# The first weight pair of each seven-product stage in the order in which its products read it, with two K pairs ahead of a barrier

## The chip, the cores and the metric

The kernel runs on one core of one Trainium2 chip. The time is the device time of one execution in microseconds. Five engines work side by side and wait for each other by semaphores: TensorE (PE) multiplies, VectorE (DVE), ScalarE (ACT) and GpSimd (POOL) do elementwise work, SyncE (SP) issues most DMAs. TensorE's clock is granted at one of two levels, 1.2 and 2.4 GHz (0.50 and 1.00 in the profile).

## The reference

One inference step of a two-layer encoder on 1024 prompt frames and 8 x 16 sample frames, 1152 tokens in all, width 1024. Each layer is a mixer and a SwiGLU FFN, each behind an RMSNorm and added to the residual x:

```python
def _rmsnorm(x, g):
    xf = x.astype(jnp.float32)
    y = xf * lax.rsqrt(jnp.mean(xf * xf, axis=-1, keepdims=True) + EPS)
    return (y * g.astype(jnp.float32)).astype(x.dtype)
...
def _swiglu(h, w_gu, w_down):
    gate, up = jnp.split(h @ w_gu, 2, axis=-1)
    return (jax.nn.silu(gate) * up) @ w_down
...
        x = x + y.astype(x.dtype)
        x = x + _swiglu(_rmsnorm(x, w['ffn_norm'][layer]), w['ffn_w_gu'][layer],
                        w['ffn_w_down'][layer]).astype(x.dtype)
```

Layer 0 mixes with gated DeltaNet and GLA and one output projection, layer 1 with chunked attention behind `h @ w['c_w_qkv']`.

## The kernel before

Activations are kept transposed: `xT` is 8 tiles of 128 rows by 1152 tokens. A float32 operand is split into a high part (a cast on ScalarE) and a low part (source minus high part, on VectorE for tokens and GpSimd for weights), and a product is three matmuls: high by high, low by high, high by low.

**Seven products.** The FFN's input projection (22 pairs of weight tiles, p = 0 to 21) and the QKV projection (12 pairs) are computed as 2 x 2 blocks in seven products instead of eight: pair p of the weights, halves of the contraction and of the 1152 tokens. Products 0 to 6 are a11 x11, S2 T2, S1 T1, S3 T3, a12 x21, a22 T4, S4 x22. S are sums of weight blocks, made by four additions on GpSimd (`make_sums`, lines 762 to 767) once a pair has come by DMA. T are sums of token blocks. A product runs over four K blocks i, of six matmuls of 288 columns each (`block_product`, line 864). `high_part` (line 774) and `low_part` (line 778) split block q of pair p; `wts.low` counts the low parts done, and each product waits for a count. A pair after the first takes 168 matmuls.

**The tokens.** For block i, VectorE makes T1 (line 567), T2 (580), T3 (583), T4 (586), and low parts of x11 (572), T2 and T1 (593). ScalarE scales x by the gain (551), after the save of x to DRAM has landed, and makes the high parts (555, 559, 563). The four later sources, products 3 to 6, are split by `high_late` (602, 604) and `low_t_late`, `low_x_late` (609, 614), four blocks each, while the first products run.

**The norm.** The sums of squares per token come by TensorE (`norm.sums`, line 466), a square root by ScalarE (`norm.root`, 483; at two of the joints behind a table load), the inverse by VectorE (`norm.invert`, 495), and three groups of matmuls spread the inverse over partitions (476), which ScalarE copies into `norm_row` (`keep_group`, 488). VectorE multiplies results by that row (lines 1516 to 1532 in the FFN, 2250 in QKV).

**Order.** Every engine runs its own instruction list, in the order in which the functions below write it; nothing is scheduled. Three joints are touched: `mixer_out` to the first FFN, with an all-engine barrier in it; the first FFN to `qkv_in_seven`; `project_add` to the second FFN. At the first, products 0 to 2 of pair 0 are computed ahead of the barrier but for the last K block of products 1 and 2, then `keep_warm(2)` (line 143). Behind the barrier, semaphores start with credits for what was done ahead. In an FFN pair, product 3 waits for `u2_done`, an addition on VectorE (1504) that stands in its list behind the previous pair's `finish`: a multiply (1536) that waits for ScalarE's silu (1353), and a low part (1538) that waits for its high part (1361). ScalarE casts the seven weight blocks of the next pair (`block(p, q)`) ahead of silu. In QKV the results of a V pair are turned by transposes between products (line 2079, up to six groups a pair), and ScalarE copies them out (2185), two copies ahead of the cast of the next pair's block 0 and two behind it. A pair's load is issued by SyncE when low part 5 of the pair before is done (line 753).

## Time and profile before

| | us |
|---|---|
| median of 3 runs | 3249.42 (3249.1 to 3250.72) |
| profiled execution | 3249.41 |
| its span, first to last instruction | 3247.8 |
| TensorE busy | 3092.3 (95%) |
| VectorE busy | 1584.2 (49%) |
| GpSimd busy | 1550.3 (48%) |
| ScalarE busy | 1038.1 (32%) |
| TensorE's mean granted clock | 0.977 |

A timeline row has start, duration, engine, line, operation, tiles, shapes, the count of merged instructions, and in brackets the idle time of the engine ahead of it with what ended it.

### The profile page before, as it was taken

The page shows a single profiled execution, that of the slowest core. Times are in us where ns is not written, and L with a number is a line of the kernel's source. Part 1 is how long each engine was busy: PE and PEld are TensorE (multiplying, and loading weights), DVE is VectorE, ACT ScalarE, POOL GpSimd, SP SyncE. Part 2 cuts the span into 40 slices and gives each one's busy share as a digit, 9 for nine tenths or more (in the row PEclk, how much of TensorE's full clock was granted, in tenths as well). Part 3 has the DMA queues.
Part 4 walks back from the last instruction along what each step waited for, and adds up shares of the span by engine and source line. Part 5 has one row for each costly group of instructions (what it writes and reads, how often), then busy time and mean ns, then how long its engine had stood idle before and what let it go on. Part 6 is the DMA issues. An engine that isn't in the chain of part 4 may idle for free. (4 is left out here: it accounts for less than half of the span.)

```text
span 3247.8 us, 67369 instructions
## 1 busy us (share of the span) xinstructions
PE 3092.3 (95%) x28530; PEld 2904.6 (89%) x28530; DVE 1584.2 (49%) x2179; ACT 1038.1 (32%) x1840; POOL 1550.3 (48%) x1182
## 2 busy tenths in 40 slices
PE   7999977888898999999999999999999999999998
PEld 6988866777798999999999999877699999999997
DVE  5650034655666545554334433466645545644323
ACT  4222132334334332231213432366524322231204
POOL 4452143444125776774363556211135776673454
PEclk8999988999899999999999999999999999999999
DMA  6222142432661322236433353566522323328241
GB/s 207 83 79 96 49 119 89 145 109 94 206 200 54 106 101 78 91 122 255 144 99 132 93 165 104 191 207 230 152 70 83 96 83 104 104 98 293 91 146 65
DMA packets 369352, 408.93 MB, mean 126 GB/s; under 512 B 28856, under 2 KB 303377, under 8 KB 368040
## 3 DMA queue, kind: packets, MB, share of 16 engines
q1 hardware_dynamic: 362216, 379.71, 35.3%
q0 software_dynamic: 6848, 25.04, 2.5%
q8 instruction: 222, 3.64, 0.5%
q14 instruction: 66, 0.54, 0.1%
HBM read 272.18 MB, written 134.60 MB: 125 GB/s over the span
## 5 line engine op out<-in xcount | busy, mean ns | idle before, releaser
L864 PE MATMUL PS<-token_block,w_block 128*128 128x288 f32 x9408 | 1269.1, 297 | 13.9 <-POOL w_block L778 6.5
L864 PEld LDWEIGHTS PS<-token_block,w_block 128*128 128x128 f32 x9408 | 1260.4, 189 | 16.8 <-POOL w_block L778 6.2
L778 POOL TENSOR_TENSOR w_block<-w_pair_raw,w_block 128x512 fp32r<-128x512 f32 x224 | 305.4, 1369 | 161.9 <-ACT w_block L774 127.9
L1267 PE MATMUL PS<-act_slot,w_down_split 128*128 128x384 f32 x1872 | 330.4, 337 | 5.1 <-DMA act_slot<-act_dram 4.0
L1267 PEld LDWEIGHTS PS<-act_slot,w_down_split 128*128 128x128 f32 x1872 | 328.1, 189 | 6.7 <-DMA act_slot<-act_dram 4.9
L778 POOL TENSOR_TENSOR w_block<-w_sum,w_block 128x512 fp32r<-128x512 f32 x168 | 229.6, 1380 | 94.0 <-ACT w_block L774 94.0
L774 ACT CAST w_block<-w_pair_raw 128x512 fp32r<-128x512 f32 x224 | 137.2, 621 | 309.0 <-PE PS L864 260.5
L774 ACT CAST w_block<-w_sum 128x512 fp32r<-128x512 f32 x168 | 99.3, 620 | 365.7 <-POOL w_sum L767 236.8
L1239 PE MATMUL PS<-token_block,w_block 128*128 128x288 f32 x1344 | 180.3, 296 | 2.7 <-issue 2.6
L1239 PEld LDWEIGHTS PS<-token_block,w_block 128*128 128x128 f32 x1344 | 179.4, 189 | 3.5 <-issue 3.0
L762 POOL TENSOR_TENSOR w_sum<-w_pair_raw 128x512 f32<-128x512 f32 x56 | 87.1, 1555 | 165.8 <-DMA w_pair_raw<-in_ffn_w_gu_dram 115.5
L405 PE MATMUL PS<-hT_high,w_split_tiles 128*128 128x384 f32 x576 | 125.0, 343 | 2.6 <-DVEq L2511 2.6
L1089 POOL CAST w_down_split<-w_down_raw 128x1024 fp32r<-128x1024 f32 (+2 forms) x32 | 28.1, 878 | 206.7 <-PE PS L1267 171.1
L1583 DVE TENSOR_TENSOR xT<-xT,PS 128x1152 f32<-128x1152 f32 x32 | 43.3, 1353 | 153.4 <-PE PS L1267 153.4
L1509 DVE TENSOR_TENSOR u<-p,PS 128x576 f32<-128x576 f32 x44 | 33.1, 751 | 159.6 <-PE PS L864 159.6
L4728 ACT ACTIVATE probs<-minus_scores,minus_max 128x640 f32<-128x640 f32 (+3 forms) x144 | 101.0, 705 | 23.1 <-DVE minus_max L4617 22.9
L3175 POOL TENSOR_TENSOR gla_k_exps<-gla_exps,gla_kT 128x896 f32<-128x896 f32 x18 | 37.0, 2079 | 145.3 <-ACT gla_exps L3595 145.3
L1574 DVE TENSOR_TENSOR xT<-xT,PS 128x576 f32<-128x576 f32 x72 | 52.6, 751 | 106.1 <-PE PS L1239 106.1
L405 PEld LDWEIGHTS PS<-hT_high,w_split_tiles 128*128 128x128 f32 x576 | 101.5, 191 | 2.9 <-POOLq L2381 2.9
L4765 POOL COPY bias_samples<-bias_near 128x384 f32<-128x384 f32 x16 | 8.1, 506 | 194.0 <-DMA bias_near<-near_dram 147.2
L764 POOL TENSOR_TENSOR w_sum<-w_sum,w_pair_raw 128x512 f32<-128x512 f32 x56 | 96.1, 1716 | 4.4
L1525 DVE TENSOR_TENSOR ffn_up<-ffn_up,norm_row 128x1152 f32<-128x1152 f32 x44 | 91.1, 2070 | 4.9 <-DVE ffn_up L1522 0.5
(467 smaller groups left out, 5557.8 us busy)
## 6 DMA issues: line engine op xcount, KB each, us to landing
w_pair_raw<-in_ffn_w_gu_dram SPq DMA_DIRECT2D x88, 512.0 KB, 5.1
act_slot<-act_dram SPq DMA_DIRECT2D x28, 1152.0 KB, 13.7
cache_kT<-kT_dram SPq DMA_DIRECT2D x8, 2048.0 KB, 11.0
cache_v<-in_cache_c_v_dram SPq DMA_DIRECT2D x64, 256.0 KB, 4.9
act_dram<-ffn_act_high SPq DMA_DIRECT2D x28, 576.0 KB, 2.8
act_dram<-ffn_act_low SPq DMA_DIRECT2D x28, 576.0 KB, 3.9
down_source<-down_dram SPq DMA_DIRECT2D x56, 288.0 KB, 5.0
xT<-xT_dram SPq DMA_DIRECT2D x24, 576.0 KB, 11.7
```

Of the source, the lines that this page charges most:

```text
L405: m = nc.tensor.matmul(PS[:, banks + j, 0:GN], wl if p == 2 else wh, sl if p == 1 else sh, start=(k == first and p == 0), stop=(k == last ...
L762: tt(self.sum_(p, 2), b0, b1, ALU.add).then_inc(self.summed, 1)
L764: tt(self.sum_(p, 1), self.sum_(p, 2), a0, ALU.subtract).then_inc(self.summed, 1)
L774: self.nc.scalar.copy(self.blocks[q][:, 0], self.source(p, q)).then_inc(self.high, 1)
L778: self.nc.gpsimd.tensor_tensor(self.blocks[q][:, 1], self.source(p, q), self.blocks[q][:, 0], ALU.subtract).then_inc(self.low, 1)
L864: m = nc.tensor.matmul(to[:, j], w, x[:, j * HN:(j + 1) * HN], start=(q < 3 and i == 0 and t == 0), stop=(q > 3 and i == 3 and t == 2), sk ...
L1239: m = nc.tensor.matmul(to[:, j], w, x[:, j * HN:(j + 1) * HN], start=(q < 3 and i == 0 and t == 0), stop=(q > 3 and i == 3 and t == 2), sk ...
L1267: m = nc.tensor.matmul(down_banks(u)[:, j], wd[u % 2][:, int(q == 2), k], x[:, int(q == 1), group(j)], start=(k == 0 and q == 0), stop=(k ...
L1525: tt(up[:], up[:], row[:], ALU.mult).then_inc(up_scaled, 1)
L1574: tt(two(x), two(x), down_tile(d, q), ALU.add).then_inc(x_down, 1)
L1583: tt(groups(xT[:, n]), groups(xT[:, n]), down_banks(u), ALU.add).then_inc(x_added, 1)
L4728: nc.scalar.activation(pr[:, g % 2, hp, 0:w], sc[:, hp, 0:w], ACT.Exp, scale=-1.0, bias=mn[:, g % 2, hp, 0:1], accum_out=sm[:, g % 2, hp, ...
```

## The change

- `make_rest` is split into `make_t2`, `make_t4` and `make_t3`, and `low_t` waits only for its own source. At every joint VectorE now goes T2, low T2, T4, low T1, T3 instead of T2, T3, T4, low T2, low T1.
- `norm.root` and `norm.invert` move ahead of the four high and low parts of product 5's source.
- ScalarE's cast of block 0 of pair 1 moves ahead of the `keep_group` copies, and GpSimd's low part of it ahead of the wait for x22's low parts and the sums of pair 1.
- In `mixer_out`, the sums of the first weight pair move ahead of square additions 2 and 3 on GpSimd; squares and weight casts are placed anew on ScalarE; VectorE takes adds 6 and 7 later.
- The last K block of products 1 and 2 (12 matmuls) moves ahead of the barrier.

```diff
     def low_t(self, dve, q, i):
         dve.wait_ge(self.high, 3 * i + (2 if q == 2 else 3))
-        dve.wait_ge(self.t_made, 4 * i + 4)
+        dve.wait_ge(self.t_made, 4 * i + (2 if q == 2 else 3))
...
         for q in wts.order[5:7]:
             wts.low_part(pool, 0, q)
+        wts.low_part(pool, 1, 0)
         tok.wait_late(pool, 6)
         for p in range(1, NP):
             wts.make_sums(pool, p)
-            for q in range(7):
+            for q in range(int(p == 1), 7):
                 wts.low_part(pool, p, q)
...
+        norm.root(act)
         for i in range(4):
             tok.high_late(act, 5, i)
-        norm.root(act)
         act.wait_ge(wts.low, 7)
         for i in range(4):
             tok.high_late(act, 6, i)
+        block(1, 0)
         for j in range(G):
             norm.keep_group(act, j)
-        for q in range(6):
+        for q in range(1, 6):
             block(1, q)
...
         middle(0)
+        norm.invert(dve)
         for i in range(4):
             tok.low_t_late(dve, 5, i)
-        norm.invert(dve)
...
     def pe_credits(pe):
-        pe.sem_inc(mm, 1)
+        pe.sem_inc(mm, 3)
...
-        for n in (1, 2, 3):
+        add_square(1)
+        pool.wait_ge(mm, LAST * KT + 2)
+        wts.make_sums(pool, 0)
+        for n in (2, 3):
             add_square(n)
         wts.low_part(pool, 0, 0)
-        pool.wait_ge(mm, LAST * KT + 2)
-        wts.make_sums(pool, 0)
...
         block_product(nc, pe, tok, wts, half_banks(PS, 0), 0, 0, range(3, 4))
+        block_product(nc, pe, tok, wts, half_banks(PS, 2), 0, 2, range(3, 4))
+        block_product(nc, pe, tok, wts, half_banks(PS, 1), 0, 1, range(3, 4))
         e.keep_warm(2)
...
-        for i in range(3):
+        for i in range(4):
             square(LAST, 2 * i)
-            square(LAST, 2 * i + 1)
-            if i == 2:
-                act.wait_ge(mm, LAST * KT + 7)
+            if i == 3:
                 for q in wts.order[1:3]:
                     wts.high_part(act, 0, q)
             act.wait_ge(x_squared, LAST * KT + 2 * i + 1)
             tok.scale(act, i)
             tok.high_x11(act, i)
-            tok.high_t1(act, i)
-            tok.high_t2(act, i)
             if i == 1:
                 act.wait_ge(mm, LAST * KT + 3)
                 wts.high_part(act, 0, 0)
-        square(LAST, 6)
-        act.wait_ge(x_squared, LAST * KT + 7)
-        tok.scale(act, 3)
-        tok.high_x11(act, 3)
-        tok.high_t1(act, 3)
+            if i < 3:
+                square(LAST, 2 * i + 1)
+            tok.high_t1(act, i)
+            tok.high_t2(act, i)
+        square(LAST, 7)
         for q in wts.order[3:5]:
             wts.high_part(act, 0, q)
-        tok.high_t2(act, 3)
-        square(LAST, 7)
...
         for i in range(4):
             if 0 < i < 3:
                 add(LAST, 2 * i)
-            if i < 3:
-                add(LAST, 2 * i + 1)
+            add(LAST, 2 * i + 1)
+            tok.make_t1(dve, i)
+            dve.wait_ge(added, LAST * KT + 2 * i + 2)
+            tok.make_t2(dve, i)
+            tok.low_x11(dve, i)
+            tok.low_t(dve, 2, i)
+            tok.make_t4(dve, i)
+            tok.low_t(dve, 1, i)
             if i == 2:
                 add(LAST, 6)
-            tok.make_t1(dve, i)
-            tok.low_x11(dve, i)
-            if i == 2:
-                add(LAST, 7)
-            dve.wait_ge(added, LAST * KT + 2 * i + 2)
-            tok.make_rest(dve, i)
-            tok.low_t(dve, 2, i)
-            tok.low_t(dve, 1, i)
+            tok.make_t3(dve, i)
```

ScalarE at the first joint ahead of the barrier, before: squares (line 4318), casts of weight blocks 1 and 2 from `w_sum`, then scale (551) and high parts of token block i = 2, then square 6.

```order
L4318 ACTIVATE x_sq_2795<-xT 128x384 x2
L774 CAST w_block_2764<-w_sum 128x512
L774 CAST w_block_2765<-w_sum_2771 128x512
L551 ACTIVATE xT<-xT,gains 128x1152
L555 CAST token_block_2728<-xT 128x576
L559 CAST token_block_2736<-token_sum_2760 128x576
L563 CAST token_block_2732<-token_sum_2756 128x576
L4318 ACTIVATE x_sq_2795<-xT 128x384
```

The same stretch of ScalarE's list after the change, from square 4 to scale 3.

```order
L4334 ACTIVATE x_sq_2795<-xT 128x384
L551 ACTIVATE xT<-xT,gains 128x1152
L555 CAST token_block_2728<-xT 128x576
L4334 ACTIVATE x_sq_2795<-xT 128x384
L559 CAST token_block_2736<-token_sum_2760 128x576
L563 CAST token_block_2732<-token_sum_2756 128x576
L4334 ACTIVATE x_sq_2795<-xT 128x384
L778 CAST w_block_2764<-w_sum 128x512
L778 CAST w_block_2765<-w_sum_2771 128x512
L551 ACTIVATE xT<-xT,gains 128x1152
```

The two casts stood ahead of scale 2 and now stand behind square 6, just ahead of scale 3.

GpSimd at the first joint behind the barrier, before: low parts of blocks 5 and 6 of pair 0, the four sums of pair 1, low parts of pair 1 (`w_block` without a number is block 0).

```order
L778 TENSOR_TENSOR w_block_2768<-w_pair_raw,w_block_2768 128x512
L778 TENSOR_TENSOR w_block_2769<-w_sum_2772,w_block_2769 128x512
L762 TENSOR_TENSOR w_sum_2774<-w_pair_raw 128x512
L764 TENSOR_TENSOR w_sum_2773<-w_sum_2774,w_pair_raw 128x512
L765 TENSOR_TENSOR w_pair_raw<-w_pair_raw 128x4x128
L767 TENSOR_TENSOR w_sum_2775<-w_pair_raw,w_sum_2773 128x512
L778 TENSOR_TENSOR w_block<-w_pair_raw,w_block 128x512
L778 TENSOR_TENSOR w_block_2764<-w_sum_2773,w_block_2764 128x512
```

The same place in GpSimd's list after the change.

```order
L782 TENSOR_TENSOR w_block_2768<-w_pair_raw,w_block_2768 128x512
L782 TENSOR_TENSOR w_block_2769<-w_sum_2772,w_block_2769 128x512
L782 TENSOR_TENSOR w_block<-w_pair_raw,w_block 128x512
L766 TENSOR_TENSOR w_sum_2774<-w_pair_raw 128x512
L768 TENSOR_TENSOR w_sum_2773<-w_sum_2774,w_pair_raw 128x512
L769 TENSOR_TENSOR w_pair_raw<-w_pair_raw 128x4x128
L771 TENSOR_TENSOR w_sum_2775<-w_pair_raw,w_sum_2773 128x512
L782 TENSOR_TENSOR w_block_2764<-w_sum_2773,w_block_2764 128x512
```

The low part of block 0 of pair 1 moved from behind the four sums to ahead of them; the other two joints read alike.

## Rows read from the trace of the kernel before

**Rows 1.** The page's engine table: busy us (share of the span) xinstructions.

```profile
PE 3092.3 (95%) x28530; PEld 2904.6 (89%) x28530; DVE 1584.2 (49%) x2179; ACT 1038.1 (32%) x1840; POOL 1550.3 (48%) x1182
```

**Rows 2.** TensorE's waits, whole span: us in total, times, longest.

```profile
PE PS L864 <- POOL w_block L778: 6.5, 4, 1.8
...
PE PS L476 <- DVE norm_by_token L495: 3.7, 3, 1.2
```

**Rows 3.** Timeline of TensorE, first joint.

```profile
1004.68 3.92 PE L864 MATMUL PS<-token_block,w_block 128*128 128x288 f32 x18 [2.90 <-DVE token_block L572]
...
1012.92 1.88 PE L143 MATMUL PS<-consts_f 128*128 128x512 f32 x4
1018.94 3.00 PE L864 MATMUL PS<-token_block,w_block 128*128 128x288 f32 x12 [4.14 <-DVEq L1723]
...
1024.12 6.64 PE L864 MATMUL PS<-token_block,w_block 128*128 128x288 f32 x48
...
1042.47 17.76 PE L864 MATMUL PS<-token_block,w_block 128*128 128x288 f32 x120 [1.85 <-POOL w_block L778]
```

**Rows 4.** Timeline of ScalarE, first joint.

```profile
977.51 1.26 ACT L551 ACTIVATE xT<-xT,gains 128x1152 f32<-128x1152 f32 x1 [1.19 <-DMA xT_dram<-xT]
...
986.76 1.26 ACT L551 ACTIVATE xT<-xT,gains 128x1152 f32<-128x1152 f32 x1 [0.93 <-DMA xT_dram<-xT]
...
998.98 1.14 ACT L774 CAST w_block<-w_sum 128x512 fp32r<-128x512 f32 x2 [2.25 <-POOL w_sum L767]
```

**Rows 5.** Timeline of VectorE, first joint ahead of the barrier.

```profile
982.92 1.43 DVE L593 TENSOR_TENSOR token_block<-token_sum,token_block 128x576 fp32r<-128x576 f32 x2 [0.46 <-DVE xT L586]
984.26 1.01 DVE L4366 TENSOR_TENSOR xT<-xT,PS 128x384 f32<-128x384 f32 x2
...
991.81 3.43 DVE L593 TENSOR_TENSOR token_block<-token_sum,token_block 128x576 fp32r<-128x576 f32 x2
...
1015.16 2.03 DVE L593 TENSOR_TENSOR token_block<-token_sum,token_block 128x576 fp32r<-128x576 f32 x2
```

**Rows 6.** Timeline of GpSimd, first joint behind the barrier.

```profile
1034.88 1.30 POOL L762 TENSOR_TENSOR w_sum<-w_pair_raw 128x512 f32<-128x512 f32 x1 [6.08 <-DVE token_block L614]
```

**Rows 7.** The chain that ended last, third joint: start, us, what.

```profile
2467.80 2.87 DVE token_block L614 x4
...
2475.89 2.35 POOL w_block L778
...
2488.17 11.83 PE PS L864 x87
```

**Rows 8.** Timeline of VectorE, third joint.

```profile
2484.97 2.39 DVE L1538 TENSOR_TENSOR ffn_act_low<-ffn_gate,ffn_act_high 128x1152 fp32r<-128x1152 f32 x1 [1.23 <-ACT ffn_act_high L1361]
2487.29 0.74 DVE L1504 TENSOR_TENSOR u<-p,PS 128x576 f32<-128x576 f32 x1
```

**Rows 9.** Timelines of TensorE, ScalarE and GpSimd, second joint.

```profile
1816.71 4.96 PE L864 MATMUL PS<-token_block,w_block 128*128 128x288 f32 x24 [1.84 <-POOL w_block L778]
...
1830.08 0.79 PE L2079 MATMUL PS<-consts_f,xT 128*128 128x128 f32 x5 [0.61 <-ACT xT L2185]
...
1829.15 0.62 ACT L774 CAST w_block<-w_pair_raw 128x512 fp32r<-128x512 f32 x1 [5.83 <-DMA w_pair_raw<-in_c_w_qkv_dram]
...
1819.62 3.75 POOL L778 TENSOR_TENSOR w_block<-w_pair_raw,w_block 128x512 fp32r<-128x512 f32 x3
```

**Rows 10.** Timeline of VectorE, first joint behind the barrier.

```profile
1022.51 0.75 DVE L1504 TENSOR_TENSOR u<-p,PS 128x576 f32<-128x576 f32 x1
...
1051.42 0.74 DVE L1504 TENSOR_TENSOR u<-p,PS 128x576 f32<-128x576 f32 x1
```

**Rows 11.** Stretch table: stretch, its us, busy by engine, granted clock, DMA.

```profile
1044.50:1046.50 2.00, 2.00 (x10) 2.00 (x10) 0.62 (x1) 1.34 (x2) 2.00 (x2) 0.50 0.00 0
```

**Rows 12.** DMA issues, 2460 to 2500 us: count, KB each, median us to landing.

```profile
w_pair_raw<-in_ffn_w_gu_dram SPq DMA_DIRECT2D x4, 512.0 KB, 5.0
```

**Rows 13.** Timeline of SyncE's DMA issues, third joint.

```profile
2464.08 23.09 SPq L753 DMA_DIRECT2D w_pair_raw<-in_ffn_w_gu_dram  x4
```

More of the change, by code:

```diff
@@ L1150, in first_pair @@
                 product(0, 2, (0, 1, 2))
-            product(0, 1, (3,))
-            product(0, 2, (3,))
-            if not seam.begun:
+                product(0, 1, (3,))
+                product(0, 2, (3,))
                 seam.wait_squares(pe)
@@ L1667, in vector @@
                 dve.wait_ge(x_added, KT + 2 * i + 2)
-                x2.make_rest(dve, i)
+                x2.make_t2(dve, i)
                 x2.low_t(dve, 2, i)
+                x2.make_t4(dve, i)
                 x2.low_t(dve, 1, i)
+                x2.make_t3(dve, i)
             add_square(KT - 1)
@@ L2056, in gpsimd @@
             wts.make_sums(pool, p)
-            for q in range(7):
+            for q in range(int(p == 1), 7):
                 wts.low_part(pool, p, q)
@@ L2194, in scalar @@
             wts.high_part(act, 0, q)
+        norm.root(act)
         for i in range(4):
             tok.high_late(act, 5, i)
-        norm.root(act)
         act.wait_ge(wts.low, 7)
@@ L2200, in scalar @@
             tok.high_late(act, 6, i)
+        block(1, 0)
         for j in range(G):
             norm.keep_group(act, j)
-        for q in range(6):
+        for q in range(1, 6):
             block(1, q)
@@ L2278, in vector @@
         middle(0)
+        norm.invert(dve)
         for i in range(4):
             tok.low_t_late(dve, 5, i)
-        norm.invert(dve)
         for i in range(4):
```

33 lines of the change are left out of this document (20 added, 13 removed).

## The prediction

> **What bounds the kernel now.** I read the engine table of the page first: TensorE is busy 95% of the span [rows 1], so a change is worth what it does to TensorE's gaps and clock and no more. Then the list of waits. The change touches three joints, where one stage hands over to a stage of seven products: the first at 977 to 1054 us (mixer output to the first FFN, with the barrier in it), the second at 1809 to 1830 (FFN to QKV), the third at 2467 to 2488 (attention output to the second FFN). At each the list shows the same two gaps: about 1.2 us before the spread of the inverse roots (3.7 in three) and 1.8 us before the first product of pair 1, which waits for a low part from GpSimd (6.5 in four, one of them elsewhere); once there is a barrier gap of 4.1 [rows 2, 3]. Those are what the edits go at. Last I read the timelines of all engines through the joints, asking at each which wait ends last, because a gap that closes early only helps if nothing behind it is tied to another engine.
>
> **First joint, ahead of the barrier.** Now: the last mixer product ends at 1000.1, TensorE waits 2.9 us for the low part of x11 block 2, computes 48 block matmuls, warms for 1.9 and is done at 1014.8 [rows 3]. VectorE is the last to arrive (1015.16 + 2.03 = 1017.2 [rows 5]); TensorE restarts at 1018.94 [rows 3], so the barrier costs 1.75 after the last arrival.
>
> I lay the new order out with durations of rows: 0.72 to 0.8 us for a VectorE operation on a 576-wide half (two in 1.43), 1.7 if GpSimd works beside it (two in 3.43), 0.5 for an add [rows 5]; 1.26 for a scale, 0.68 for a high part, 0.57 for a weight cast [rows 4]; 1.3 for a GpSimd operation [rows 6], 1.6 beside VectorE.
> - GpSimd's four sums, which ran at 992.8, now follow square 1. ScalarE takes that square behind scale 0 and its high part (977.5 + 1.3 + 0.7 [rows 4]), so the sums run at about 981 to 988. They meet VectorE in block 0, which was then uncontended: five operations go from 0.75 to about 1.6. Adds 2 and 3, at 984.3 now [rows 5], come at 988.2.
> - Scale 1 waits for the save of x that this add releases, some 2 us (984.7 to 986.76 [rows 4, 5]): 990.7. Block 1's seven VectorE operations, three beside GpSimd's low part and squares, end at 998.9; adds 4 and 5 at 999.8; scale 2 again waits for its save, 1001.4. T2 stands ahead of the low part of x11, so block 2 of a11 x11 is ready at 1005.7 (1004.68 now).
> - The decisive move: the casts of weight blocks 1 and 2 ran at 998.98 [rows 4], ahead of scale 2. They now stand behind square 6, which waits for add 6, which VectorE takes only after the low part of T1 in block 2: add 6 at 1008.4, square 1008.9, two casts 1010.0, two low parts 1012.4. The products S2 T2 and S1 T1 both wait for that. TensorE has nine block steps left, 54 matmuls of 0.135 us (48 in 6.64 [rows 3]) and about 1.4 more at the half clock after the wait (12 matmuls took 3.00 instead of 1.6 after the barrier gap [rows 3]): 1021.1, and 1.9 of warming: 1023.0. The last arrival moves from 1017.2 to 1023.0: **+5.8 us**. The two moved K pairs (12 matmuls) are in this.
> Bounds: with no slowing between VectorE and GpSimd the same layout ends at 1016.4, a gain of 0.8; with operations of both slowed as in the worst pair of rows it ends 1 us later, +6.8. I stay at 5.8, since the 3.43 us for two [rows 5] is from this very stretch.
>
> The Trainium skill (SBUF — State Buffer, Who interferes with whom) says that a VectorE instruction with two SBUF inputs and a GpSimd instruction that reads SBUF exclude each other for a whole instruction. The 3.43 us agree roughly; full alternation by that rule would put the end another 1 to 2 us later.
>
> **Behind the barrier, first joint.** The sums of squares follow at once, but product 3 waits for u2, which was ready 4.3 us behind the restart (1022.51 + 0.75 - 1018.94 [rows 3, 10]; casts, low parts, the add) and will be again, so of the 3.0 us of moved matmuls only about 0.8 are gained there. The root and the inverse are then early, the 1.2 us gap goes; low part (1,0) is early, and the 1.85 us gap [rows 3] goes. But product 3 of pair 1 waits for its u, and that hangs on another chain: last low part of x22 to four GpSimd sums (1034.88 on [rows 6]) to six casts, table load, silu, multiply, high part, low part and u at 1051.42 + 0.74 = 1052.2 [rows 10]. TensorE reached that product at 1042.47 + 17.76 - 6.7 = 1053.5 [rows 3], so the slack is only 1.35 us. The chain does not get shorter. GpSimd takes low part (1,0) as soon as the weights have landed and are cast, about 1033.5 if the load takes 5 us as at the third joint [rows 12], and ends about when the sums could start; and VectorE's multiplications by the norm row, which fell on GpSimd's low parts (2.35 instead of 1.29, [rows 7]), now fall on the sums: +1.1 and +0.5. Less 0 to 0.9 for a low part that may run uncontended, u is ready 0.6 to 1.5 later; the joint ends 0 to +0.1 against now, and TensorE then has a gap of 2 to 3 us before the product. A gap of 1.85 brought the granted clock to 0.50, the 1.2 GHz level, for about 3 us [rows 3, 11]; now this price is paid at the first product of pair 1, later at the fourth, perhaps on top of one at the second. I take **+1.0** (0 to 1.8).
>
> **Third joint.** The same chain without slack: low parts of x22 end at 2470.67, sums at 2475.89 [rows 7]; low part 2.39, u at 2487.29 + 0.74 = 2488.03 [rows 8]; TensorE's product starts at 2488.17 [rows 7]. Weights of pair 1 land 5 us (the median) after their issue at 2464.1 and about 0.5 later [rows 12, 13], near 2469.7. Then cast and low part (1,0) occupy GpSimd till about 2471.8: the sums start 1.1 later, and meet the two multiplications, +1.6 at most; the low part of the activations runs freer, -0.9. u comes 1.8 later. A new gap of some 3 us before the product costs between nothing and 1.4 in clock. **+2.2** (+1 to +4).
>
> **Second joint.** There is no silu here, but TensorE's fifth transpose group waits for a row copy behind the cast of pair 2's first block, which waits for its load (1829.15, released by the DMA); TensorE waits 0.61 [rows 9]. The load is issued once GpSimd has done low part (1,5), at 1819.62 + 3.75 = 1823.4 [rows 9]. GpSimd's operations to there are the same ten, but the sums start some 0.8 late behind low part (1,0) (an estimate from the third joint, whose loads take the same 5 us), wait 0.6 for a cast behind them, and the low part taken ahead, 1.3, goes off the end: load about +0.3 with the stretching by VectorE the same. TensorE's earlier arrival turns into about 4.5 us of waiting, and the half clock behind it (24 matmuls in 4.96 for 3.3, [rows 9], paid at pair 1 now and included in today's arrival) is paid again behind the wait: **+1.8** (0 to +2.3).
>
> Orders of T2, T4, T3 in the second and third joint cost nothing: TensorE runs 72 block matmuls there without a gap; the cover is gone only if the low part of T1 moved by more than some 3 us, and it moves forward.
>
> **Sum.** 5.8 + 1.0 + 2.2 + 1.8 = +10.8 us. The profiled execution took 3249.41 (span 3247.8), the median is 3249.42, so they can be used alike: 3260.2.
>
> **Rivals.**
> - *Light contention at the first joint* (0.20): sums and VectorE overlap little, as the 1.3 us rows on GpSimd would allow; the barrier moves by 0 to 2.5 instead of 5.8; 3250 to 3256, centre 3254.
> - *Gaps close and nothing replaces them* (0.07), on the other side. The mechanism is the low part (1,0) in pair 1: if the weights land so early that it ends before the low parts of x22, and if the chain to u has 2 us more room than I read, TensorE keeps 1.2 + 1.8 us a joint and about 1.5 of clock at two. That gives -12, and with the barrier coming 5.8 later, -6; with a neutral barrier 3238. It decides for faster where u in pair 1 is done before TensorE's third product ends.
> - *Worse* (0.08): half clock after each of TensorE's new waits ahead of the barrier and behind it, 3265 to 3270.
> - *No change* (0.03): the last arrival at the barrier stays VectorE's.
> The forecast itself has 0.62, with a range of its own of 3255 to 3264.
>
> **Numbers.** Range 3253 to 3265: the forecast, most of the light rival; left out are the worse one's end and the faster side. What a measurement here tells from no change is 0.2%, 6.5 us. Slower by more, from 3255.9: 0.59 of the forecast, 0.05 of the light rival, 0.08 of the worse one, 0.72. The same: 0.03, 0.14 and no change's 0.03, 0.20. Faster: 0.01 of the light rival and 0.07, 0.08.
>
> **What would show it.** The first matmul of S2 T2 at about 1012 instead of 1006; the restart behind the barrier near 1024.7; gaps before the spread and before pair 1 gone; new waits of TensorE, on VectorE's u at the fourth product of pair 1 (first and third joint), on ScalarE's row copy at the second. I am wrong if the casts of blocks 1 and 2 are done by 1004, or if TensorE enters the fourth product without a wait.

## The result, and the profile after

The changed kernel took 3267.99 us, the median of 8 runs (3257.4 to 3269.62), against 3249.26 for the kernel before beside it (8 runs, 3238.78 to 3255.41): a ratio of 1.0061, 95% interval 1.0046 to 1.0075. It is slower, as forecast, and by more than the range allowed (3253 to 3265). The profiled execution took 3267.39 us, its span 3265.8, and TensorE was busy for 3094.8 us of it (3092.3 before [rows 1]); the loss is waiting, and clock.

Where TensorE waits at the joints (all of the span: us in total, times, longest):

```profile
PE PS L868 <- POOL w_block L782: 12.5, 5, 5.3
...
PE PS L868 <- DVE u L1509: 5.8, 2, 2.9
...
PE PS L2091 <- ACT xT L2197: 4.4, 1, 4.4
```

The wait for the inverse [rows 2] is gone from the list, the waits for `w_block` have doubled, and two new ones have come: for u, and for ScalarE's row copy (`xT` at line 2197). Timeline of TensorE through the first joint:

```profile
1006.22 1.06 PE L868 MATMUL PS<-token_block,w_block 128*128 128x288 f32 x6 [4.10 <-DVE token_block L572]
1012.57 9.72 PE L868 MATMUL PS<-token_block,w_block 128*128 128x288 f32 x54 [5.30 <-POOL w_block L782]
1022.13 1.88 PE L143 MATMUL PS<-consts_f 128*128 128x512 f32 x4
1025.73 2.14 PE L466 MATMUL PS<-consts_f,norm_row 128*128 128x1 f32 x18 [1.72 <-PEq L114]
1030.15 8.68 PE L868 MATMUL PS<-token_block,w_block 128*128 128x288 f32 x48 [2.28 <-issue]
...
1043.77 6.62 PE L868 MATMUL PS<-token_block,w_block 128*128 128x288 f32 x48
1052.95 6.64 PE L868 MATMUL PS<-token_block,w_block 128*128 128x288 f32 x48 [2.56 <-POOL w_block L782]
1062.50 3.69 PE L868 MATMUL PS<-token_block,w_block 128*128 128x288 f32 x16 [2.91 <-DVE u L1509]
```

S2 T2 starts behind a wait of 5.3 us; the restart behind the barrier is the row at 1025.73; product 3 waits 2.28 us for u2, and the 48 matmuls of products 3 and 4, one row, then take 8.68 us where they took 6.64 [rows 3]. The row at 1043.77 is product 6 of pair 0 and the first product of pair 1, which begins at 1047.0 without a gap; pair 1 waits for 2.56 us before its second product and 2.91 before its fourth (24 matmuls a product). VectorE and ScalarE ahead of the barrier, one timeline:

```profile
979.18 1.57 DVE L572 TENSOR_TENSOR token_block<-xT,token_block 128x576 fp32r<-128x576 f32 x1
980.68 1.85 DVE L597 TENSOR_TENSOR token_block<-token_sum,token_block 128x576 fp32r<-128x576 f32 x1
982.45 1.84 DVE L584 SCALAR_TENSOR_TENSOR xT<-xT,gains,token_sum 128x576 f32<-128x576 f32 x1
984.39 1.66 DVE L597 TENSOR_TENSOR token_block<-token_sum,token_block 128x576 fp32r<-128x576 f32 x1
985.98 1.85 DVE L590 SCALAR_TENSOR_TENSOR xT<-xT,gains 128x576 f32<-128x576 f32 x1
987.75 1.00 DVE L4376 TENSOR_TENSOR xT<-xT,PS 128x384 f32<-128x384 f32 x2
...
1008.34 0.55 DVE L4376 TENSOR_TENSOR xT<-xT,PS 128x384 f32<-128x384 f32 x1
...
1009.35 1.12 ACT L778 CAST w_block<-w_sum 128x512 fp32r<-128x512 f32 x2
...
1010.83 1.25 ACT L551 ACTIVATE xT<-xT,gains 128x1152 f32<-128x1152 f32 x1 [0.36 <-DMA xT_dram<-xT]
...
1018.36 1.85 DVE L590 SCALAR_TENSOR_TENSOR xT<-xT,gains 128x576 f32<-128x576 f32 x1
```

Five operations of block 0 take 1.57 to 1.85 us each beside GpSimd's first square addition and four sums (978.8 to 987.2), adds 2 and 3 come at 987.75, add 6 at 1008.34, and behind its square the two casts of blocks 1 and 2. VectorE's last operation ends at 1020.2, nearly four us ahead of TensorE's warming (1022.13 + 1.88). The second and third joint, timelines of TensorE:

```profile
1842.43 1.30 PE L2091 MATMUL PS<-consts_f,xT 128*128 128x128 f32 x5 [4.44 <-ACT xT L2197]
...
2496.94 6.66 PE L868 MATMUL PS<-token_block,w_block 128*128 128x288 f32 x48 [2.40 <-POOL w_block L782]
...
2506.48 1.78 PE L868 MATMUL PS<-token_block,w_block 128*128 128x288 f32 x6 [2.89 <-DVE u L1509]
```

**How executions are compared here.** Absolute times shift from execution to execution by more than the change is worth: the first joint starts between 965 and 976 us, though no edit stands ahead of it. The kernel before alone was timed at 3230 to 3262 us in the runs beside the experiments. So I measure inside each joint. In the first, zero is VectorE's first `xT<-xT,PS` addition of the last token group (970.98 in the first execution of the kernel before, 969.68 after); "the restart" is TensorE's first matmul behind the barrier; "behind" is from there to u3 of pair 4 (u3 is the second addition into `u`, line 1509 before, and product 5 waits for it). The second joint is from the first matmul of pair 0 to the eight transposes behind pair 2's run of 120 matmuls, the third from the first matmul of pair 0 to u3 of pair 4. Each is the difference of two rows.

| kernel | restart | last to arrive | behind | ratio, 95% |
|---|---|---|---|---|
| before, two executions | 47.96, 47.75 | VectorE 46.2, 46.0 | 105.3, 108.4 | |
| changed | 56.05 | TensorE 54.3 | 108.8 | 1.0061 (1.0046-1.0075) |
| 1 mixer part alone | 55.90 | TensorE 54.2 | 106.8 | 1.0017 (0.9995-1.0040) |
| 2 all but the mixer part | 47.54 | VectorE 45.8 | 112.0 | 1.0007 (0.9991-1.0023) |
| 3 casts 1, 2 back | 54.19 | TensorE 52.5 | 106.6 | 1.0021 (1.0005-1.0036) |
| 4 no early low part | 56.20 | TensorE 54.5 | 107.1 | 1.0020 (1.0009-1.0030) |
| 5 casts 1, 2 and sums back | 52.62 | TensorE 50.9 | 110.0 | 1.0031 (1.0016-1.0046) |
| 6 before + 12 matmuls ahead | 53.60 | TensorE 51.9 | 106.5 | 1.0019 (1.0007-1.0031) |
| 7 before + early root | 47.74 | VectorE 46.0 | 105.7 | 1.0004 (0.9984-1.0024) |
| 8 changed + warming | 55.63 | TensorE 53.9 | 106.3 | 1.0031 (1.0019-1.0042) |
| 9 12 matmuls back | 53.84 | TensorE 52.1 | 106.7 | 1.0040 (1.0018-1.0062) |
| 10 casts 1, 2, sums, 12 back | 52.45 | GpSimd 50.7 | 110.3 | 1.0036 (1.0013-1.0058) |
| 11 add 6 back | 52.60 | TensorE 50.9 | 109.7 | 1.0027 (1.0007-1.0046) |
| 12 add 6 and 12 back | 51.98 | GpSimd 50.2 | 106.8 | 1.0028 (1.0014-1.0043) |
| 13 as 10, add 6 back too | 50.73 | GpSimd 48.9 | 110.7 | 1.0007 (0.9987-1.0026) |
| 14 as 13, casts 3, 4 back too | 50.71 | VectorE 49.0 | 104.4 | 1.0014 (0.9987-1.0040) |
| 15 before, T3 behind barrier | 47.05 | VectorE 45.3 | 107.6 | 0.9993 (0.9976-1.0010) |
| 16 before, more warming | 47.69 | VectorE 45.9 | 105.7 | 0.9991 (0.9976-1.0006) |
| 17 both | 47.25 | VectorE, TensorE 45.5 | 106.4 | 0.9990 (0.9975-1.0006) |

Arrivals are counted like the restart, from the first add; each ratio is to the kernel before timed beside that kernel. In every row the restart is 1.72 to 1.78 us behind the last of the four arrivals. That makes the column of arrivals the thing to read: it names the engine that set the barrier. Kernels 5, 1 and 2 show that the ratios alone would not do: restarts of 52.6, 55.9 and 47.5 stand beside 1.0031, 1.0017 and 1.0007, with intervals that overlap.

### The profile page after: what moved, and what is told of

It reads as the page before. It is cut to its first block and busy times, and to the rows that moved or that the text cites. A ratio compares the mean times of both kernels' runs of the same rounds, so it can differ in the third digit from the quotient of the medians.

```text
span 3265.8 us, 67368 instructions
## 1 busy us (share of the span) xinstructions
PE 3094.8 (95%) x28530; PEld 2908.7 (89%) x28530; DVE 1590.4 (49%) x2179; ACT 1036.9 (32%) x1840; POOL 1544.1 (47%) x1182
## 5 line engine op out<-in xcount | busy, mean ns | idle before, releaser
L782 POOL TENSOR_TENSOR w_block<-w_pair_raw,w_block 128x512 fp32r<-128x512 f32 x224 | 295.0, 1322 | 188.2 <-ACT w_block L778 152.0
L1579 DVE TENSOR_TENSOR xT<-xT,PS 128x576 f32<-128x576 f32 x72 | 52.6, 751 | 106.1 <-PE PS L1243 106.1
```

The lines of the kernel that those rows point to most:

```text
L782: self.nc.gpsimd.tensor_tensor(self.blocks[q][:, 1], self.source(p, q), self.blocks[q][:, 0], ALU.subtract).then_inc(self.low, 1)
L1579: tt(two(x), two(x), down_tile(d, q), ALU.add).then_inc(x_down, 1)
```

## The experiments

**Before again.** The kernel before, unchanged.

> The kernel before, unchanged, for a second execution in the trace. Theory E (how long the granted clock stays at 0.50 behind a gap differs from execution to execution of one and the same list): the half clock behind the barrier, 3.4 us in the first execution, has another length here, up to the 10 us seen with the old part ahead of the barrier in the changed kernel. Rival F (the lists decide it): 3 to 4 us again, and the stretch from the restart to the fifth u3 is 105.3 us again.

Its TensorE timeline behind the barrier:

```profile
1015.82 2.83 PE L864 MATMUL PS<-token_block,w_block 128*128 128x288 f32 x12 [3.99 <-DVEq L1723]
1018.45 3.83 PE L466 MATMUL PS<-consts_f,norm_row 128*128 128x1 f32 x18
1022.15 8.60 PE L864 MATMUL PS<-token_block,w_block 128*128 128x288 f32 x48
```

Stretch table of the same execution (us, TensorE busy, granted clock, DMA):

```profile
1016.00:1018.00 2.00, 2.00 (x11) 0.59 0.04 8
1022.00:1024.00 2.00, 2.00 (x10) 0.50 0.00 0
1025.00:1027.00 2.00, 2.00 (x11) 0.60 0.54 152
```

The same list that ran products 3 and 4 in 6.64 us [rows 3] runs them here in 8.60: the clock stays at 0.50, the 1.2 GHz level, for 10.2 us instead of 3.4, and "behind" is 3.1 us longer. Theory E holds. A single trace therefore can't say that products 3 and 4 at half clock belong to the change. The two executions were taken at different times, but kernels 13 and 14 below, timed side by side and with one list behind the barrier, differ in the same way: 8.79 and 6.63 us for these 48 matmuls.

**1 and 2, the mixer part alone, and all but it.** Kernel 1 is the kernel before with the change's part ahead of the barrier; kernel 2 is the changed kernel with the old part.

```diff
 # kernel 2, against the changed kernel
-        block_product(nc, pe, tok, wts, half_banks(PS, 2), 0, 2, range(3, 4))
-        block_product(nc, pe, tok, wts, half_banks(PS, 1), 0, 1, range(3, 4))
         e.keep_warm(2)
...
```

> The kernel before with the first joint's part ahead of the barrier taken from the change (order of sums, squares, casts, adds, the 12 moved matmuls), all else as before. Theory A (late casts set the barrier, and TensorE's wait for u2 plus the half clock behind it delays the chain to u of pair 1): restart behind the barrier 26.0 us behind the first add of the last group (56.0 in the changed kernel, 48.0 before, counted from 970), a wait of about 2.3 us ahead of product 3 of pair 0 and 48 matmuls in 8.7 us behind it; whole kernel +9 to +11 us. Rival B (what was lost behind the barrier comes from the early low part and root): the 12 matmuls moved ahead give back about 0.8, product 3 runs at full clock, 6.6 us; whole kernel +7 us.

> The changed kernel with the old part ahead of the barrier (12 matmuls behind the barrier again). Theory A: the restart stands as in the kernel before, product 3 of pair 0 is entered without the wait for u2 and at full clock (48 matmuls in 6.6 us); behind the barrier the first joint costs +0.5 to +1.5, the second +2, the third +2.5; whole kernel +5 to +6 us. Rival B: the first joint costs +3.5 behind the barrier here too, whole kernel +8 us.

Kernel 1 restarts at 55.90, and kernel 2 at 47.54: all 8 us ahead of the barrier are the mixer part's. In kernel 1 the 48 matmuls of products 3 and 4 run in 8.59 us behind the 2.28 wait, as A says; but kernel 2, with no wait for u2, ran them in 8.42 at a half clock of 10.2 us, which A excluded, so the wait is not needed for it:

```profile
1030.04 8.42 PE L868 MATMUL PS<-token_block,w_block 128*128 128x288 f32 x48
```

That was why the kernel before was traced again. Whether the wait makes it likelier is open: with the 12 matmuls ahead of the barrier and no warming added, all seven executions took 7.9 to 8.8 us for these 48; with the 12 behind it, seven of twelve took 8.1 to 9.4 and five 6.5 to 6.6. The whole kernels can't tell A from B: the intervals of 1.0017 and 1.0007 reach from -2 to +13 and from -3 to +7 us.

**3 and 5, casts back, then sums back too.** ScalarE's casts of blocks 1 and 2 ahead of scale 2; then GpSimd's sums behind square additions 2 and 3.

```diff
-            if i == 3:
+            if i == 2:
+                act.wait_ge(mm, LAST * KT + 7)
                 for q in wts.order[1:3]:
                     wts.high_part(act, 0, q)
```

> The changed kernel with only the casts of weight blocks 1 and 2 put back ahead of ScalarE's scale 2. Theory A (these casts are what holds S2 T2): S2 T2 is entered without the 5.3 us wait, at 1006 to 1008, VectorE becomes the last to arrive (about 1020), and the restart moves from 1025.7 to 1021 to 1022; whole kernel 4 to 5 us shorter than the changed one, +4 to +7 against before. Rival C (VectorE and GpSimd slow each other, and the joint is late for that alone): the casts give at most 1 us.

> The changed kernel with the casts of weight blocks 1 and 2 ahead of scale 2 and GpSimd's four sums of pair 0 behind square additions 2 and 3 and the low part, both as before; VectorE's new order and the moved 12 matmuls stay. Theory C (the early sums slow VectorE's first blocks, and that remains once the casts are back): adds 2 and 3 return from 18 to 13.5 us behind the first add of the last group, the restart from 54.2 to 47 to 49 us behind it (47.96 before); whole kernel 5 to 7 us shorter than with the casts alone. Rival G (VectorE's own new order of T2, low parts and adds is what is slow): the restart stays above 52.

TensorE in kernel 3:

```profile
1009.46 9.38 PE L868 MATMUL PS<-token_block,w_block 128*128 128x288 f32 x48 [1.06 <-POOL w_block L782]
1020.13 1.06 PE L868 MATMUL PS<-token_block,w_block 128*128 128x288 f32 x6 [1.30 <-DVE token_block L597]
```

Theories A and C both missed. The wait ahead of S2 T2 shrinks from 5.3 to 1.06 us in kernel 3, but the restart moves by 1.9 and not by about 4: TensorE then waits again, at its last six matmuls, for the low part of T1 of the last block. With the sums back, adds 2 and 3 return to 13.6 and the restart moves by another 1.6 only, to 52.62, not to 47 to 49; that is rival G's "above 52", though the 12 matmuls are in it too. The late casts are one of several holds of nearly the same length.

**6 and 9, the 12 matmuls alone, and all but them.**

> The kernel before with only the 12 block matmuls of products 1 and 2 moved ahead of the barrier. The restart stays at 48 us behind the first add of the last group, since TensorE has 2.4 us to spare there. Theory A: the 3.0 us saved behind the barrier turn into a wait for u2 of about 2.3 us and half clock behind it; product 3 starts at most 0.8 us earlier and ends 0 to 1.5 us later than before; whole kernel 0 to +2 us. Rival H (the move is a gain that the other edits hide): no half clock, whole kernel -1 to -3 us.

> The changed kernel with only the 12 matmuls back behind the barrier. Theory N (two mechanisms overlap: the late casts hold TensorE to 1020 by themselves, the moved matmuls need VectorE's last low parts and would hold it nearly as long): the restart comes 53.5 to 55 us behind the first add of the last group (56.05 with both, 53.6 with the 12 matmuls alone, 47.96 without either), so each alone costs some 6 us and both together 8. Rival P (the 12 matmuls are nearly all of it): 48 to 50.

TensorE in kernel 6, where nothing else is changed:

```profile
1015.05 3.25 PE L864 MATMUL PS<-token_block,w_block 128*128 128x288 f32 x12 [3.44 <-DVE token_block L593]
1018.10 3.39 PE L143 MATMUL PS<-consts_f 128*128 128x512 f32 x4
1023.22 2.75 PE L466 MATMUL PS<-consts_f,norm_row 128*128 128x1 f32 x18 [1.73 <-PEq L114]
```

I had written that TensorE has 2.4 us to spare there, and expected the restart to stay at 48. It has them, and can't use them: the last K block of S2 T2 and S1 T1 needs VectorE's last low parts, its last operation ahead of the barrier (1013.64 + 2.03 = 1015.67). So these 12 matmuls and the warming behind them come after VectorE, at half clock (3.25 and 3.39 us instead of 1.6 and 1.88), and TensorE is the last to arrive, at 51.9 instead of 43.8. Alone the move costs 5.7 us at the restart. Behind it product 3 starts at 4.42 us and not at 5.18 or 6.32, as told for u2; to u3 of pair 4 it is 106.5, between the 105.3 and 108.4 of before, so a gain there can't be read. Kernel 9 shows that the other edits without it cost 5.9 to 6.1: theory N, two holds that overlap, and together make 8.

**10, 13 and 14, down to VectorE's order.** From the changed kernel with casts 1 and 2, sums and the 12 matmuls as before (10), to add 6 ahead of T1 of block 2 again (13), to the casts of blocks 3 and 4 between the high parts of T1 and T2 of the last block (14). The diff is add 6's move, in 13 and 14.

```diff
             add(LAST, 2 * i + 1)
+            if i == 2:
+                add(LAST, 6)
             tok.make_t1(dve, i)
...
             tok.low_t(dve, 1, i)
-            if i == 2:
-                add(LAST, 6)
             tok.make_t3(dve, i)
```

> The changed kernel with sums, casts and the 12 matmuls all as before in the first joint; only VectorE's order and the rest of ScalarE's stay new there. Theory Q (the new order of VectorE is harmless ahead of the barrier): restart at 47 to 49 us behind the first add of the last group. Rival R (it delays VectorE's last operation by itself, since T3 of the last block and adds 6 and 7 stand later): 50 or above.

> The kernel with sums, casts of blocks 1 and 2 and the 12 matmuls as before, and add 6 as before too; VectorE's order of T2, T4, T3 and low parts, the squares and the casts of blocks 3 and 4 stay new. Theory W (several chains of like length end at the barrier, each edit lengthens one, and the longest counts): T1 of the last block starts at about 40.0 behind the first add of the last group (42.6 with add 6 late, 38.2 before), GpSimd ends last at about 48.1, restart at 49.5 to 50.3. Rival X (the early sums are not in it): 51.5 or above.

> The same with the casts of weight blocks 3 and 4 back between the high parts of T1 and T2 of the last block. Theory W: GpSimd's last addition ends 1 to 1.4 us earlier, VectorE is the last to arrive again, restart at 48.3 to 49.3 (47.75 to 47.96 before). Rival Y (GpSimd's arrival is not what sets it): as e16.

There "e16" is kernel 13.

Kernel 10, timeline of ScalarE, VectorE and GpSimd:

```profile
1007.45 0.55 DVE L4375 TENSOR_TENSOR xT<-xT,PS 128x384 f32<-128x384 f32 x1
...
1009.96 1.25 ACT L551 ACTIVATE xT<-xT,gains 128x1152 f32<-128x1152 f32 x1 [1.40 <-DMA xT_dram<-xT]
...
1011.24 0.76 DVE L567 TENSOR_TENSOR token_sum<-xT 128x576 f32<-128x576 f32 x1 [2.04 <-ACT xT L551]
...
1017.81 1.50 POOL L4275 TENSOR_TENSOR norm_row<-norm_row,x_sq 128x384 f32<-128x384 f32 x1
```

Rival R of kernel 10 holds: the restart is at 52.45, though nothing but VectorE's order, the squares and the casts of blocks 3 and 4 are new. Here the route of add 6 is seen whole: add 6 at 1007.45, the save of that tile, scale 3 released by the DMA at 1009.96, T1 of the last block at 1011.24 behind 2.04 us of waiting. And GpSimd is the last to arrive (1017.81 + 1.50), because the casts of blocks 3 and 4 stand behind square 7 and its two low parts behind them. With add 6 back (13) the last block starts 1.7 us earlier (40.9 behind the first add) and the restart is 1.7 earlier, at 50.73, 0.4 above what theory W allowed and below rival X. With casts 3 and 4 back too (14) GpSimd is done 1.3 us earlier, and nothing is gained: its low parts now meet VectorE's last block, and VectorE is the last, at 49.0. I had expected 48.3 to 49.3; it is 50.71. What stays, 2.8 us, goes with VectorE's new order, and with ScalarE's new order of squares and high parts, which no kernel here puts back alone. Kernel 14, timeline of VectorE, T1 of block 2 and T1 of block 3:

```profile
1004.66 0.76 DVE L567 TENSOR_TENSOR token_sum<-xT 128x576 f32<-128x576 f32 x1 [3.43 <-ACT xT L551]
...
1013.90 0.74 DVE L567 TENSOR_TENSOR token_sum<-xT 128x576 f32<-128x576 f32 x1
```

That is 9.24 us for block 2 where it took 8.05 (30.33 to 38.38 behind the first add); block 2 also starts 1.35 us later, and the last block takes 0.2 longer: together the 2.8. How much of it is which engine's order isn't shown.

**11 and 12, add 6 back alone, and with the 12 matmuls back.**

> The changed kernel with only VectorE's add 6 back ahead of T1 of block 2. Theory S (add 6 releases the save of x tile 6, the save releases scale 3, and scale 3 starts all of the last token block; square 6 and the two casts stand in the same line): scale 3 starts at 35 to 37 us behind the first add of the last group instead of 41.2, S2 T2 is entered with at most 1 us of waiting, and what is left is the price of the 12 moved matmuls, which wait for VectorE's last low parts: restart at 51 to 53.6 instead of 56.05. Rival T (the loss is spread over contention and order): 55 or above.

> The same with the 12 matmuls back behind the barrier too. Theory S: nothing that matters is left of the loss ahead of the barrier although sums, casts, squares and the order of T2, T4, T3 and low parts are all as changed: restart at 47.5 to 49.5 (47.75 and 47.96 before). Rival T: 52 or above.

Kernel 11, timeline of ScalarE (scale 3) and TensorE:

```profile
1003.85 1.25 ACT L551 ACTIVATE xT<-xT,gains 128x1152 f32<-128x1152 f32 x1
...
1006.85 9.09 PE L868 MATMUL PS<-token_block,w_block 128*128 128x288 f32 x54 [2.04 <-POOL w_block L782]
...
1015.77 1.88 PE L143 MATMUL PS<-consts_f 128*128 128x512 f32 x4
```

Scale 3 starts 4.1 us earlier (37.1), S2 T2 is entered 2.8 earlier, still behind a wait of 2.04 where theory S had at most 1, and the restart comes at 52.60, within theory S's 51 to 53.6: of all single edits that were put back, this one takes back most, 3.5 of 8.1 us. But T1 of the last block starts at 42.5 as in the changed kernel (42.4): VectorE comes to it no sooner, since the early sums have made it late from block 0 on (adds 2 and 3 at 18.0, 13.3 before). So the gain went through the casts, which stand behind square 6, and not through scale 3: the number was hit by another route than theory S's. Kernel 12 misses its 47.5 to 49.5: GpSimd is the last again, with VectorE close behind. Timeline of VectorE, GpSimd and TensorE in kernel 12:

```profile
1014.40 1.82 DVE L590 SCALAR_TENSOR_TENSOR xT<-xT,gains 128x576 f32<-128x576 f32 x1
...
1015.56 1.50 POOL L4275 TENSOR_TENSOR norm_row<-norm_row,x_sq 128x384 f32<-128x384 f32 x1
...
1018.84 1.86 PE L868 MATMUL PS<-token_block,w_block 128*128 128x288 f32 x12 [2.79 <-DVEq L1731]
```

Against kernel 13 (50.73), kernel 12 has the early sums and the late casts of blocks 1 and 2: 1.25 us.

**4 and 7, the early low part of pair 1 taken out, and the root and the inverse alone.**

```diff
 # kernel 4, against the changed kernel
-        wts.low_part(pool, 1, 0)
...
-            for q in range(int(p == 1), 7):
+            for q in range(7):
...
-        block(1, 0)
```

> The changed kernel without the early cast and low part of block 0 of pair 1, at all three joints. Theory A (that low part delays the four sums and with them u of pair 1): the wait of 1.8 us ahead of pair 1 is back, the sums start 1.1 us earlier at the third joint, the wait for u shrinks from 2.9 to 0 to 1; third joint +0.5 to +1 instead of +2.7, second 0 to +1 instead of +2.1; whole kernel 2 to 4 us shorter than the changed one. Rival D (the multiplications that now meet the sums are what lengthens the chain): u comes no earlier, the gap of 1.8 comes on top, and the kernel takes 0 to 3 us longer than the changed one.

> The kernel before with only the root and the inverse moved ahead of the four high and low parts of product 5's source, at all three joints. Theory L (pair 1 is pinned by GpSimd's four sums, whatever TensorE gains ahead of them): the 1.23 us gap before the spread is gone, the gap before pair 1 grows from 1.8 to 3.0 or more, pair 1 starts 29.8 to 30.3 us behind the start of pair 0 at the third joint as before (29.6 to 29.8), and u of pair 1 comes 0.5 to 1.3 us later than the 38.6 to 38.8 of before, since the inverse stands ahead of the low parts that release the sums; whole kernel 0 to +3 us. Rival M (a closed gap is time won): pair 1 starts at 28.5 at the third joint, whole kernel -3 us.

TensorE at the third joint in kernel 4, the first product of pair 1:

```profile
2494.92 5.37 PE L868 MATMUL PS<-token_block,w_block 128*128 128x288 f32 x27 [3.76 <-POOL w_block L782]
```

The same place in kernel 7:

```profile
2477.03 5.25 PE L864 MATMUL PS<-token_block,w_block 128*128 128x288 f32 x27 [3.75 <-POOL w_block L778]
```

With the root and the inverse early the gap before the spread is gone in both, and the gap before pair 1 has grown from 1.76 to 3.75: pair 1 starts 30.3 us behind pair 0, against 29.6 to 29.8. Nothing is won, theory L, and the whole kernel 7 stays where it was (1.0004). Theory A of kernel 4 had this gap at 1.8 again; the wait for u behind it is gone, as it said. Counted from the first matmul of pair 0, u of pair 1 starts at 38.6 to 38.8 in the seven executions with the old lists there, at 40.0 in kernels 4 and 7, and at 40.9 to 41.8 with everything: 1.3 us are the early inverse and root, 1.3 the early low part. Kernel 4 has the new order of T2, T4 and T3 and kernel 7 the old one, so that order costs nothing there. At the second joint the early low part is all of the loss: kernel 4 takes 59.91 us there, as before (59.99), the changed one 62.11.

**8, 16, 15 and 17, the clock, and a try at something better.** Kernel 8 puts warming matmuls in the wait for u2; 16 doubles the warming of the kernel before; 15 moves T3 of the last block behind the barrier; 17 does both.

```diff
 # kernel 15, against the kernel before
+        if seam.begun:
+            tok.make_t3(dve, 3)
         for i in range(4):
             tok.low_t_late(dve, 3, i)
...
 # kernel 16, against the kernel before
-        e.keep_warm(2)
+        e.keep_warm(4)
```

> The changed kernel with four records (1.88 us) of warming matmuls behind the sums of squares, in the place of most of the 2.28 us wait for u2 ahead of product 3. Theory A (that wait is what lowers the clock for product 3): the 48 matmuls go in 6.6 to 7.2 us instead of 8.68, and the joint ends 1.5 to 2 us earlier. Rival J (the clock has fallen already for the barrier's gap and the 18 narrow matmuls behind it): product 3 takes 8 us or more again.

> The kernel before with eight records of warming ahead of the barrier instead of four (3.8 us instead of 1.9), so that TensorE is done at 45.8 behind the first add of the last group, still before VectorE (46.2), and the gap shrinks from 4.1 to 2.2. Theory U (the gap brings the clock down): no half clock behind the barrier, the 12 matmuls in 1.7 instead of 3.0, product 3 in 6.6, the stretch from the restart to the fifth u3 103 to 104 us instead of 105.3 to 108.4. Rival V (the 18 narrow matmuls behind the barrier bring it down too): half clock of 3.4 us or more again.

> The kernel before with one operation moved: VectorE's T3 of the last block, 1.89 us beside GpSimd and not read before product 3, goes from ahead of the barrier to the first place behind it. If VectorE is the last to arrive and its list decides, the restart comes 0.8 to 1.9 us earlier than 47.96 behind the first add of the last group, u2 comes at most 0.4 us later relative to the restart, which product 3 does not wait for, and the whole kernel is 1 to 2 us shorter, which the traces can show and the times hardly. Rival: what is saved ahead is a longer wait for the sums of pair 1, or TensorE's warming is the last to arrive: 0.

> The kernel before with T3 of the last block moved behind the barrier and eight records of warming: restart at 46.5 to 47.3, gap 1.75 to 2.2 us. Theory U: as for the run with the warming alone, so 2 to 5 us faster than before over the joint. Rival V: only the 0.9 us of T3.

In kernel 8 products 3 and 4 take 7.30 us: between the two answers, with a half clock that was over sooner (3.4 us), which one execution can't tell from chance. The added warming itself ran at half clock, 3.66 us, and put product 3 off by 0.3. TensorE behind the barrier in kernel 16:

```profile
1019.90 3.25 PE L864 MATMUL PS<-token_block,w_block 128*128 128x288 f32 x12 [2.45 <-DVEq L1723]
```

And in kernel 17:

```profile
1012.55 1.85 PE L882 MATMUL PS<-token_block,w_block 128*128 128x288 f32 x12 [1.77 <-DVEq L1743]
1014.23 2.06 PE L466 MATMUL PS<-consts_f,norm_row 128*128 128x1 f32 x18
1017.11 9.35 PE L882 MATMUL PS<-token_block,w_block 128*128 128x288 f32 x48 [0.81 <-issue]
```

Theory U falls: the gap went from 4.1 to 2.45 and 1.77 us, and the clock fell all the same, at once in 16, and in 17 in the further gap of 0.81 us ahead of product 3. T3 behind the barrier does what it should, the restart is 0.7 to 0.9 us earlier in kernel 15, and u2 0.1 later. The three kernels lie at 0.9990 to 0.9993 with intervals that take in 1: not slower, and not shown to be faster.

## Why the prediction was right and wrong

Averaged over the executions that share the lists in question, the terms are: at the restart 47.75 (before, before again, 2, 7: 47.5 to 48.0) to 55.95 (changed, 1, 4, 8: 55.6 to 56.2), **+8.2** for a forecast of +5.8; behind it 106.56 (before, before again, 7, 15, 16) to 108.39 (changed, 2, 3, 5 and 8 to 14), **+1.8** for +1.0, where single executions reach from 104.4 to 112.0; second joint 60.06 (before, before again, 1, 6, 15 to 17) to 62.01 (the same eleven), **+2.0** for +1.8; third joint, the same kernels, 112.24 to 113.60, **+1.4** for +2.2. The sum is 13.3 us where 10.8 was forecast. Only the restart and the second joint repeat closely enough to be read to a few tenths; for "behind" and the third joint the two means differ by 1.8 and 1.4 with a 95% interval (an estimate from the scatter of the executions) of about 2.0 and 1.4 either way. (Kernels 7 and 15, in the mean for "behind", have one edit there each.)

- **The restart is the term that failed**: +5.8 was forecast, 8.2 measured. In the changed kernel itself the path was the one told, late casts, S2 T2, 54 matmuls, warming; its steps were mis-sized. The five operations of block 0 took 1.57 to 1.85 us and not 1.6, so adds 2 and 3 came at 18.1 behind the first add (forecast 17.2), add 6 at 38.7 (37.4), and the first matmul of S2 T2 at 42.9 (41.4). The 54 matmuls took 9.72 us, not 8.7: 1.4 us had been set aside for the clock, and it stood at 0.50 for the first 5 us of them.
- **What it was put down to** failed too: "the decisive move: the casts" named one hold out of several. Put back alone they return 1.9 us; the 12 matmuls alone cost 5.7. I had counted their own 1.6 us ("in this") and put the wait for VectorE's last low parts at nothing. In the changed kernel that wait is covered, since those low parts are done before TensorE comes to them; it counts as soon as the casts are back. I followed the latest chain to its end, and not the next one below it.
- **The slowing of VectorE beside GpSimd** was right in kind. The operations of block 0 that took 0.7 to 0.8 us take up to 1.85. The Trainium skill (SBUF — State Buffer, Who interferes with whom) has a VectorE instruction with two SBUF inputs and a GpSimd instruction that reads SBUF contend for a shared port pair, which is an exclusive lock. By that rule, the trace agrees in kind: VectorE's 1.85 is its own 0.81 and 1.04 of a GpSimd operation of 1.30 [rows 6], not the whole of it. I had kept full alternation, "another 1 to 2 us", out of the sum; S2 T2 started 1.5 late.
- **Behind the barrier** the steps stood as told: u2 was ready 4.3 us behind the restart (3.57 + 0.75 in nearly all executions), 0.8 us were gained up to product 3, the gaps before the spread and before pair 1 went, and TensorE waited 2.91 us at the fourth product of pair 1. Not in the sum was that products 3 and 4 would run at half clock. The run of before again shows that they do so without the change as well; of the 3.4 us seen between the first two traces the means leave 1.8. (The recorded 0.6 to 1.5 for u should read 0.7 to 1.6 by its own terms: 1.1 + 0.5, less 0 to 0.9.)
- **Joints two and three** went by the named mechanism: 4.44 us for the row copy ("about 4.5"), 2.89 for u ("some 3"). u came 2.6 us later and not 1.8: 1.3 by the low part for a forecast of 1.1, and 1.3 by root and inverse where 0.7 was left for the multiplications; but the first execution of the kernel before had no half clock behind its gap before pair 1, which the other executions mostly have, so the joint as a whole lost less, 1.4.
- **The rivals.** *Light contention* is out by the five slowed operations, *no change* by TensorE's arrival behind VectorE's, *gaps close and nothing replaces them* because u in pair 1 is not done before TensorE wants it in any kernel with the early low part (waits of 1.4 to 2.9 us). *Worse*, with 0.08, is the one whose 3265 to 3270 holds the measured time, and its mechanism is seen in part: in the changed kernel's profiled execution the clock falls to 0.50 in the wait ahead of S2 T2, at u2, at u in pair 1, at the row copy and at u in the third joint, 30.6 us at half clock in the three joints against 13.6 and 20.5 in the two executions of the kernel before. What these cost is inside the terms above; it doesn't add to them.

**Left open.** The joints sum to 13.3 us, and by them alone the kernel would take some 3263 us, inside the stated range; the timed ratio says 15 to 24. So the restart's 2.4 us are nearly all by which the joints exceed the forecast sum, and they don't explain why the timed median lies at 3268. In the two profiled executions the span grew by 18.0 us: 8.1 at the restart, 3.4 behind it, 2.1 and 3.7 at the second and third joint, and 0.7 net in all other stretches; the terms behind the restart and of the third joint lie above their means. Kernel 8, the changed kernel with one warming call more (four records), was timed at 1.0031 (6 to 14 us), which fits the joints better, and kernels 1 and 2, whose edits together are the change, at 1.0017 and 1.0007. The eight timed runs of the changed kernel list a mean granted clock of 0.974 to 0.976, kernel 8's ten 0.972 to 0.978 with a mean 0.002 higher, so the clock may be part of it; that isn't shown. Where the changed kernel's other 5 us were I can't place.

## What to carry to other kernels

Ahead of a barrier, list the arrival of every engine and not only of the last: here TensorE, GpSimd and VectorE arrived at 54.3, 51.4 and 50.5, and putting one edit back uncovered the next hold. Work moved into an engine's idle time must be checked for what it reads: 12 matmuls put into a gap waited for the very operation that ended it, and cost 5.7 us. And an early start ahead of a wait that another engine pins (four sums on GpSimd) only moves the wait by a product (from ahead of pair 1 to ahead of its second and fourth product).

## What the runs showed of the hardware

- One and the same list had TensorE's clock at 0.50 for 3.4 us behind the barrier in one execution and for 10.2 in another, 3.1 us in the end. Executions with the gap at 2.45 us (kernel 16) and at 1.77 and a further 0.81 (kernel 17) had it too. The stretches at 0.50 in the joints of all 20 executions lasted 3.4, 6.8, 10.2 or 13.7 us.
- From the last arrival at the barrier to TensorE's restart it was 1.72 to 1.73 us where TensorE came last (nine executions), 1.75 where VectorE did (eight), 1.78 where GpSimd did (three).
- Stretches that no edit touched differed by as much as the change: from u3 of pair 4 to the second joint 652.2 to 665.4 us in 20 executions, mostly 662 to 664. Only differences inside a joint could be read to a few tenths.
